# Identity turns split into two row tiles in a two-layer state-space and attention trunk

## The reference

```
h = x
for layer in 0, 1:
    if layer == 1: k, v = rms(h) @ w_kv                     # shared keys and values
    h += 0.5 * swiglu(rms(h), w_in, w_out)                  # hidden width 2816
    h += s5_mixer(rms(h)) if layer == 0 else attention(rms(h) @ w_q, k, v) @ w_o
    h += 0.5 * swiglu(rms(h), w_in, w_out)
return rms(h)
```

## Time and profile before

| | |
|---|---|
| median of 3 runs | 1004.16 us (1003.1 to 1004.64) |
| the profiled execution, first to last instruction (its span) | 1002.6 us |
| TensorE busy | 965.9 us, 96% |
| VectorE busy | 591.7 us, 59% |
| ScalarE busy | 484.5 us, 48% |
| GpSimd busy | 247.9 us, 25%, nearly all before 250 us |
| mean granted TensorE clock | 0.992 of full speed |
| data moved | 169.31 MB, 169 GB/s |

### The profile page before, as it was taken

How to read it: one execution, slowest core, us unless ns; L and a number is a source line. 1 busy time by engine, 2 the same in 40 slices (tenths; PEclk the granted TensorE clock), 3 DMA queues, 4 the chain that set the end, 5 groups by cost and what they waited for, 6 DMA issues and landing times.

```text
span 1002.6 us, 14413 instructions
## 1 busy us (share of the span) xinstructions
PE 965.9 (96%) x5728; PEld 799.7 (80%) x5728; DVE 591.7 (59%) x724; ACT 484.5 (48%) x688; POOL 247.9 (25%) x308
## 2 busy tenths in 40 slices
PE   5999999988799999999999999999999999999996
PEld 4888888777688888888888888888887788888885
DVE  4666765679666555555556555554556565555553
ACT  6544444342256544445463445444457554454441
POOL 4999989899200000000000000000050000000000
PEclk9999999999899999999999999999999999999999
DMA  9666666600065665576666666666661265666651
GB/s 338 216 186 191 185 189 178 197 27 4 24 187 186 190 179 187 183 210 178 200 180 185 188 183 189 188 187 192 183 178 61 87 190 187 185 188 178 188 164 42
DMA packets 47890, 169.31 MB, mean 169 GB/s; under 512 B 5968, under 2 KB 5968, under 8 KB 47824
## 3 DMA queue, kind: packets, MB, share of 16 engines
q1 hardware_dynamic: 46368, 166.74, 54.9%
q10 hardware_dynamic: 1456, 1.66, 0.5%
HBM read 167.33 MB, written 1.05 MB: 168 GB/s over the span
## 4 chain that ended last, share of the span: by engine, by line
PE 90%; POOL 5%; DVE 2%; DMA 1%; ACT 1%; issue 1%; SPq 0%; POOLq 0%; DVEq 0%; ACTq 0%
PE ps L995 86%; POOL w_bd L452 2%; PE ps L1006 2%; POOL c_bd L463 2%; DMA h<-in_x 1%; POOL decay L470 1%; PE ps L1019 1%; PE ps L1212 1%; DVE w_lo L748 1%; PE ps L1032 0%; ACT w_hi L521 0%; ACT act_out L638 0%; ACT act_out L559 0%; SPq L285 0%; DVE fin L988 0%
## 5 line engine op out<-in xcount | busy, mean ns | idle before, releaser
L748 DVE TENSOR_TENSOR w_lo<-raw,w_hi 128x1024 fp32r<-128x1024 f32 x312 | 402.1, 1291 | 278.7 <-ACT w_hi L521 278.0
L521 ACT ACTIVATE w_hi<-raw 128x1024 fp32r<-128x1024 f32 x312 | 329.7, 1059 | 270.5 <-PE ps L995 270.5
L995 PE MATMUL ps<-w_hi,x_hi 128*128 128x512 f32 x896 | 355.3, 396 | 11.0 <-DVE w_lo L748 10.9
L995 PE MATMUL ps<-w_hi,x_lo 128*128 128x512 f32 x896 | 350.5, 391 | 0.0
L995 PE MATMUL ps<-w_lo,x_hi 128*128 128x512 f32 x896 | 349.9, 391 | 0.0
L995 PEld LDWEIGHTS ps<-w_hi,x_hi 128*128 128x128 f32 x896 | 169.0, 189 | 45.2 <-issue 11.2
L995 PEld LDWEIGHTS ps<-w_hi,x_lo 128*128 128x128 f32 x896 | 168.8, 188 | 36.0
L995 PEld LDWEIGHTS ps<-w_lo,x_hi 128*128 128x128 f32 x896 | 169.1, 189 | 33.7
L333 POOL TENSOR_TENSOR ms<-ss 128x2 f32<-128x2 f32 x7 | 1.4, 200 | 720.3 <-ACT act_out L559 718.6
L995 PE MATMUL ps<-w_hi,hid_hi 128*128 128x512 f32 x352 | 137.6, 391 | 0.0
L995 PE MATMUL ps<-w_hi,hid_lo 128*128 128x512 f32 x352 | 137.1, 389 | 0.0
(11 more groups left out here) (115 smaller groups left out, 634.6 us busy)
## 6 DMA issues: line engine op xcount, KB each, us to landing
raw<-in_in SPq DMA_DIRECT2D x176, 512.0 KB, 4.2
raw<-in_out SPq DMA_DIRECT2D x88, 512.0 KB, 3.6
raw<-in_glu SPq DMA_DIRECT2D x16, 512.0 KB, 4.1
raw<-in_k SPq DMA_DIRECT2D x8, 512.0 KB, 4.5
raw<-in_v SPq DMA_DIRECT2D x8, 512.0 KB, 4.4
raw<-in_q SPq DMA_DIRECT2D x8, 512.0 KB, 4.5
raw<-in_o SPq DMA_DIRECT2D x8, 512.0 KB, 4.2
xt<-in_xt SPq DMA_DIRECT2D x4, 256.0 KB, 6.3
```

Source lines behind the costliest of these rows:

```text
L521: act.activation(w_hi[:, gu % WS, :], raw[:, gu % RAW, :], ACT.Copy)\
L748: dve.tensor_tensor(w_lo[:, gu % WS, :], raw[:, gu % RAW, :], w_hi[:, gu % WS, :].bitcast(F32), ALU.subtract)\
L995: return pe.matmul(o, w, x, start=start, stop=stop, skip_group_check=True)
```

## The change

A turn of 128 tokens becomes two turns of 64: rows 0 to 63 of the tile with the identity's rows and columns 0 to 63, then rows 64 to 127 with its other corner. The stationary operand of each is 64 x 128, 64 columns stream, and the result is 128 channels by 64 tokens. The two halves go to two neighbouring banks. Banks 4 to 7 thereby become two pairs, (4, 5) and (6, 7), which all turns share; the last q block uses banks 2 and 3 for one of its two groups. Readers take both banks with one access pattern; only the `x_lo` step of DVE becomes two instructions, one for each token tile. Turns of the S5 stage (1120, 1184) and `turn_output` (1239) stay as they are.

```diff
+        PAIR = (4, 6)
+        def kq_pair(p, b, c):
+            return 2 if p.name == "q" and (b, c) == (1, 1) else PAIR[c]
+        def halves(a):
+            return a.rearrange("p (b h x) -> p b h x", h=2, x=HP)
+        def turned_halves(at, col, w):
+            return ps[:, at:at + 2, col:col + w].rearrange("p h (b x) -> p b h x", x=HP)
...
-                act.activation(hid_hi[:, 2 * b:2 * b + 2, :].rearrange("p f x -> p (f x)"),
-                               ps[:, KT + hb % 2, :], ACT.Copy).then_inc(hid_hi_done, 1)
+                act.activation(halves(hid_hi[:, 2 * b:2 * b + 2, :].rearrange("p f x -> p (f x)")),
+                               turned_halves(PAIR[hb % 2], 0, HB), ACT.Copy)\
+                   .then_inc(hid_hi_done, 1)
...
+                elif by_halves:
+                    for q in range(TT):
+                        ins = dve.scalar_tensor_tensor(lo[:, q], src[:, q], gains[:, gain, d:d + 1],
+                                                       hi[:, q], ALU.mult, ALU.subtract)
...
+            def turn(at, col, src):
+                for r in range(2):
+                    rows = slice(HP * r, HP * r + HP)
+                    last = pe.transpose(ps[:, at + r, col:col + HP], src[rows, :], ident[rows, rows])
+                return last
...
-                        last = pe.transpose(ps[:, KT + hb % 2, f * TOK + q * P:f * TOK + q * P + P],
-                                            prod[:, hb % 2, q, f * P:f * P + P], ident[:, :])
+                        last = turn(PAIR[hb % 2], (2 * f + q) * HP,
+                                    prod[:, hb % 2, q, f * P:f * P + P])
...
             def turn_kq(p, b):
...
+                    if p.name == "k" and b == 0:
+                        pe.wait_ge(x_ready, bank_read[4, c + 2])
...
             def scores(i):
-                pe.wait_ge(kq_ready, 4 + i // 2 + 1)
+                pe.wait_ge(kq_ready, 6 if i == 0 else 4 + i // 2 + 1)
...
             def turn_probs(i):
                 pe.wait_ge(exp_done, 4 * (i + 1))
                 if i == 0:
-                    pe.wait_ge(kq_drained, phases[9].kq0 + 2 * TT)
+                    pe.wait_ge(kq_ready, 8)
...
-                        last = pe.transpose(ps[:, 2 + g, a * P:a * P + P],
-                                            pr[:, i % 2, g, a * P:a * P + P], ident[:, :])
+                        last = turn(2, SW // 2 * g + a * HP, pr[:, i % 2, g, a * P:a * P + P])
```

More of the change, by code:

```diff
@@ L18 @@
 P = 128
+HP = P // 2
 TOK = 256
@@ L569, in high_x @@
                         d = 2 * c + i
-                        act.activation(x_hi[buf][:, d, :],
-                                       ps[:, TA + turned[n, c] % 2, i * TOK:i * TOK + TOK],
+                        act.activation(halves(x_hi[buf][:, d, :]),
+                                       turned_halves(PAIR[turned[n, c] % 2], P * i, P),
                                        ACT.Copy, scale=gains[:, gain, d:d + 1]).then_inc(x_hi_done, 1)
@@ L712, in pt_copy @@
                 for g in range(2):
-                    act.activation(pt[:, i % 2, g, :], ps[:, 2 + g, 0:SW], ACT.Copy)\
+                    act.activation(halves(pt[:, i % 2, g, :]), turned_halves(2, SW // 2 * g, SW // 2),
+                                   ACT.Copy)\
                        .then_inc(pt_ready, 1)
@@ L756, in block_done, with low_x @@
                     dve.wait_ge(unit_used, p.unit0 + (b + 1) * p.upb)
-            def low_x(src, dst, d, gain=None):
+            def low_x(src, dst, d, gain=None, by_halves=False):
                 tally["x"] += 1
                 dve.wait_ge(x_hi_done, tally["x"])
+                lo, hi = dst[1][:, d, :], dst[0][:, d, :].bitcast(F32)
+                if by_halves:
+                    lo, hi = halves(lo), halves(hi)
                 if gain is None:
-                    ins = dve.tensor_tensor(dst[1][:, d, :], src, dst[0][:, d, :].bitcast(F32),
-                                            ALU.subtract)
-                else:
-                    ins = dve.scalar_tensor_tensor(dst[1][:, d, :], src, gains[:, gain, d:d + 1],
-                                                   dst[0][:, d, :].bitcast(F32),
+                    ins = dve.tensor_tensor(lo, src, hi, ALU.subtract)
+                elif by_halves:
+                    for q in range(TT):
+                        ins = dve.scalar_tensor_tensor(lo[:, q], src[:, q], gains[:, gain, d:d + 1],
+                                                       hi[:, q], ALU.mult, ALU.subtract)
+                else:
+                    ins = dve.scalar_tensor_tensor(lo, src, gains[:, gain, d:d + 1], hi,
                                                    ALU.mult, ALU.subtract)
@@ L774, in low_turned @@
                     for i in range(2):
-                        low_x(ps[:, TA + turned[n, c] % 2, i * TOK:i * TOK + TOK],
-                              (x_hi[buf], x_lo[buf]), 2 * c + i, gain)
+                        low_x(turned_halves(PAIR[turned[n, c] % 2], P * i, P),
+                              (x_hi[buf], x_lo[buf]), 2 * c + i, gain, True)
             def gated(p, b):
@@ L798, in low_hidden @@
                 dve.wait_ge(hid_hi_done, hb + 1)
[L799 to L802, removed]
+                dve.tensor_tensor(halves(hid_lo[:, 2 * b:2 * b + 2, :].rearrange("p f x -> p (f x)")),
+                                  turned_halves(PAIR[hb % 2], 0, HB),
+                                  halves(hid_hi[:, 2 * b:2 * b + 2, :].rearrange("p f x -> p (f x)")
+                                         .bitcast(F32)), ALU.subtract).then_inc(hid_ready, 1)
             def residual(p, b):
@@ L827, in turned_kq @@
                     dst = (k_sb if p.name == "k" else q_sb)[:, d:d + 2, :]
-                    dve.tensor_scalar(dst.rearrange("p f x -> p (f x)"), ps[:, KT + c, :],
+                    dve.tensor_scalar(halves(dst.rearrange("p f x -> p (f x)")),
+                                      turned_halves(kq_pair(p, b, c), 0, HB),
                                       1.0 if p.name == "k" else HD ** -0.5, None, ALU.mult)\
@@ L1018, in turn_h @@
                         d = 2 * c + i
-                        last = pe.transpose(ps[:, TA + t % 2, i * TOK + q * P:i * TOK + q * P + P],
-                                            h[:, q, d * P:d * P + P], ident[:, :])
+                        last = turn(PAIR[t % 2], (2 * i + q) * HP, h[:, q, d * P:d * P + P])
                 last.then_inc(h_turned, 1)
@@ L1031, in turn_kq @@
                             a = (2 * c + i) * P
-                            last = pe.transpose(ps[:, KT + c, i * TOK + q * P:i * TOK + q * P + P],
-                                                kq[:, q, a:a + P], ident[:, :])
+                            last = turn(kq_pair(p, b, c), (2 * i + q) * HP, kq[:, q, a:a + P])
                     last.then_inc(kq_turned, 1)
```

## The result

| | first comparison | second comparison |
|---|---|---|
| before | 1004.4 us (4 runs) | 1004.59 us (28 runs) |
| the change | 1012.41 us (4 runs, 1009.18 to 1015.76) | 1010.06 us (12 runs, 1007.63 to 1015.63) |
| ratio, with its 95% interval | 1.0075 [1.0049, 1.0101] | 1.0047 [1.0022, 1.0071] |

Slower, as forecast. The runs of the change spread over 8 us, and those of the kernel before over as much (1002.43 to 1010.65), so the profile has to say what belongs to the change.

A forecast was written before the change was run, and what follows sets the result against it. TensorE was taken as the bound, 90% of the chain. 48 groups of four at +0.13 (+6.2), nine of eight at -0.07 (-0.6) and attention -1.8 gave +3.8 on 1004.16: 1008.0 us, range 1003.5 to 1012.

The forecast's parts named there:

- the two gains: Time given back on TensorE: nine groups of eight turns, -0.6 us, and the attention, -1.8 us.
- The switch: Around groups on 64 rows: each change empties the array for 0.09 us and exposes a load; +0.13 per group of four.
- The pair: Two half turns on TensorE run side by side and cost 0.057 us, for 0.108 of a whole turn.
- Groups of eight: Nine groups, six of `turn_h` and three of `turn_kq`: 1.27 us each against 1.33, -0.07 unrounded, together -0.6.
- The attention: Steps 0 to 5, scores directly ahead of `turn_probs`: no added switch, six steps of 0.3 gained, -1.8 us.
- DVE's split: `x_lo` in the dense phases as sixteen halves: about 4.2 us for 3.23, +1.0, hidden by 1.4 us of slack.
- The first: Rival: the switch costs the turns nothing, 320 turns stream faster, -16.6 us, 987.5 us; 9% with one side free included.
- the second: Rival: a pair of half turns costs 0.11 us, not 0.057, 17.6 us more, 1025.6 us; 8%.
- the fourth: Rival: DVE or ACT becomes late at the phase boundaries, six places at up to 1 us, up to 1014; 4%.
- The third, near balance: Rival: a group of four costs 0.10 instead of 0.13, the attention gives 2.5; +1.7, 1005.9 us; 16%.

The follow-up runs named there:

- fillers: The changed kernel with turns of the identity into an unread bank where TensorE idles: 1010.24 us; the kernel before with the same: 1006.43 us.
- the switch run: The changed kernel with groups of four whole again and one pair of half turns ahead of each hidden group: 1021.20 us, one execution.
- the doubled turns: The changed kernel with every half turn of the hidden groups done twice: 1020.67 us, one execution; a hidden group 1.30 us for 1.05.

## Why the prediction was right, and which terms were off

The direction and the mechanism were right: the switches outweigh the faster turns. The size was 1.7 us short of the longer comparison (+3.8 for +5.5), because the two gains were put too high and the clock had no term. The first comparison's +8 lies at the end of the range mostly by the luck of the clock.

- **The switch** (0.66 us around any group on 64 rows, +0.13 for a group of four). Right, and partly by luck. To the second dense start it is 1.046 against 0.900, +0.146 in all 44 hidden groups, where the forecast's rows gave 1.03. About 0.016 comes back in the dense matmuls behind, which the forecast didn't count: from six dense starts ahead of a hidden group to twelve behind it pass 4.693 us on average, where 4.564 passed before. That is +0.129, 48 times, +6.2 us.
- **The pair** at 0.057. A little small: 0.063. On four pairs this is the 0.02 by which the 1.03 was low.
- **Groups of eight** at -0.07. Mis-sized by the same 0.005 or 0.006 on eight pairs. Around the first one of the changed kernel, which answers to the earlier trace rows:

```profile
480.60 0.39 PE L1015 MATMUL ps<-w_hi,hid_lo 128*128 128x512 f32 x1
...
481.90 0.40 PE L1015 MATMUL ps<-w_lo,hid_hi 128*128 128x512 f32 x1
```

1.30 against 1.33 is -0.03; over the nine groups -0.3 in place of -0.6.
- **The attention** at -1.8 measured -1.25. A step from scores to scores, in the kernel before (from 767.92 in the earlier trace rows: 3.17 us), and then in the changed one:

```profile
771.09 0.93 PE L995 MATMUL ps<-k_sb,q_sb 64*128 64x128 f32 x8
```

```profile
777.03 0.93 PE L1015 MATMUL ps<-k_sb,q_sb 64*128 64x128 f32 x8
777.79 0.53 PE L1020 MATMUL ps<-ident,pr 64*128 64x64 f32 x12
...
779.96 0.93 PE L1015 MATMUL ps<-k_sb,q_sb 64*128 64x128 f32 x8
```

2.93 us, a gain of 0.24, not 0.31. The turns start 0.76 us behind the scores where it was 0.86, so 0.10 is won there and not 0.15, and six pairs at 0.063 take 0.04 more than forecast. Nor did all six steps gain: four won 0.24 or 0.25 each, and the attention up to the third step 0.29, where the forecast had two steps of 0.3. The first turns' start stayed where DVE's copy of q holds it, as forecast (3.93 us behind the stretch's start, 3.86 before):

```profile
770.47 0.58 PE L1020 MATMUL ps<-ident,pr 64*128 64x64 f32 x12 [0.52 <-DVE q_sb L847]
```

- **DVE's split** hidden. Right, with its size: sixteen halves take 4.23 us (4.2 estimated, 3.23 before), and no wait for DVE appears on TensorE in phases 2 to 9 of the changed kernel's profile.

```profile
513.82 4.23 DVE L782 SCALAR_TENSOR_TENSOR x_lo<-ps,gains,x_hi 128x128 fp32r<-128x128 f32 x16 [0.68 <-ACT x_hi L583]
517.96 3.49 DVE L762 TENSOR_TENSOR w_lo<-raw,w_hi 128x1024 fp32r<-128x1024 f32 x3
```

- **What had no term**: the clock behind the attention, +1.6 us where it falls. With it, 6.2 - 0.3 - 1.25 + 1.6 is +6.2; the longer comparison gave +5.5, whose executions need not all have the fall. With fillers, which keep the clock up, it was +3.8 where the terms without the clock give +4.65. The missing 0.85 is likely the S5 stage, by one profile of each: 72.03 us in the changed kernel's with fillers, 73.02 in the other's, whose clock there was 0.93 against 0.98. The first comparison's +8 holds bad luck of the S5 stage besides.
- **Rivals.** The first fell to the switch run, the second to the doubled turns, the fourth to the rows of DVE. The third, near balance, is only just outside the interval of the longer comparison (1.0022 at its low end); what rules it out is that a group of four costs 0.129 and not 0.10, and that the attention gave 1.25 and not 2.5.

## What to carry to other kernels

In this kernel half turns in two row tiles cost 0.063 us a pair for 0.109 a whole turn, but going to 64 rows and back costs 0.09 us of emptying on each side and uncovers two weight loads, 0.31 us in all (0.129 and four times 0.046). They pay from about seven turns a group, or where the neighbours use 64 rows already. A stretch behind an idle one can run at the lower clock: here a unit took 4.4 us for 2.8 behind waits of 0.60 and 1.02 us. So read the granted clock for the stretch that follows, and compare kernels over many executions.

## What the runs showed that I had not expected

- The kernel before has a spread of 8 us that is TensorE's clock. Its stage with idle stretches (55.60 us busy of 70.57) ran at 0.90 of full speed in its profile, and at 0.78 to 0.90 in those of the changed kernels without fillers, whose stage is the same code. 104 filler turns in the stage's idle time brought it to 1.00, the spread to 0.7 us over six executions, and the median down by 4.2 us in the comparison that had both.
- The order of half turns among themselves hardly matters: 1.059 us for four and four, 1.046 for pairs.
- A gain in front of a critical stretch can be given back by the clock: 1.0 us won in the attention, 1.5 lost in the unit behind it. Whether the half turns cause the fall isn't shown.
